# A layer kernel's block products: operands of x, gated features and norm's sums of squares made at other places

## What is computed

```python
xn = rms_norm(x, norm_mix_w)
rq, rk, rv, rg, cq, ckv, kpe, ga, gb = split_columns(xn @ w_in)
ret_y, mla_y, new_state = mixer_core(rq, rk, rv, q, ckv, kpe, w_ukv)
ret_branch = (head_group_norm(ret_y, ret_gn_w).astype(x.dtype) * jax.nn.silu(rg)) @ w_ret_o
mla_branch = mla_y @ w_mla_o
merged = jax.nn.sigmoid(ga) * ret_branch + jax.nn.sigmoid(gb) * mla_branch
h = x + merged @ w_out
g, u = jnp.split(rms_norm(h, norm_ffn_w) @ w_gate_up, 2, axis=-1)
h = h + (jax.nn.silu(g) * u) @ w_down
```

## Time and profile before

| | |
|---|---|
| time, median of 3 runs | 2125.3 us (2124.85 to 2125.86) |
| profiled execution | 2124.33 us, its span 2122.5 us |
| mean granted clock of TensorE in it | 0.970 |
| PE busy | 1985.1 us, 94% of the span |
| DVE, ACT, POOL busy | 1322.6, 799.2, 669.6 us |
| moved by DMA | 302.41 MB, 142 GB/s |

### The profile page before, as it was taken

The page is one execution under the profiler, slowest core; times in us unless marked ns, Lnnn a source line. Parts: engine busy times, 40 slices in busy tenths (PEclk is TensorE's granted clock), DMA queues, the critical chain, the costliest instruction groups (busy, mean ns, idle before and its releaser), DMA issues.

```text
span 2122.5 us, 34897 instructions
## 1 busy us (share of the span) xinstructions
PE 1985.1 (94%) x13994; PEld 1914.6 (90%) x13994; DVE 1322.6 (62%) x1982; ACT 799.2 (38%) x1390; POOL 669.6 (32%) x509
## 2 busy tenths in 40 slices
PE   8989999999897989998999979679999999999997
PEld 8878888789886979998999979679999999999997
DVE  6567776764554645977877897765656565532257
ACT  5334444441232235554554425543444343310010
POOL 0110000001332434755242665844444445200000
PEclk9999999999998999999999989889999999999998
DMA  7301011151343465669655684123232322563412
GB/s 304 109 24 34 21 34 34 32 213 36 137 139 123 157 222 195 245 245 334 219 200 203 206 305 153 46 83 113 94 112 100 106 104 102 220 258 127 168 58 85
DMA packets 121296, 302.41 MB, mean 142 GB/s; under 512 B 14128, under 2 KB 31472, under 8 KB 112944
## 3 DMA queue, kind: packets, MB, share of 16 engines
q1 hardware_dynamic: 121136, 300.18, 40.0%
HBM read 201.88 MB, written 98.25 MB: 141 GB/s over the span
## 4 chain that ended last, share of the span: by engine, by line
PE 69%; DVE 13%; DMA 5%; POOL 4%; issue 4%; ACT 2%; SPq 2%; DVEq 0%; ACTq 0%; POOLq 0%
PE ps L1127 21%; PE ps L1129 21%; PE ps L1128 21%; DVE s_lo L2078 1%; DVE tmp L2085 1%; DVE t_lo L2078 1%; PE ps L1228 1%; PE ps L1320 1%; SPq L1002 1%; PE ps L1222 1%; DVE hg L2440 1%; DVE hg L2432 1%; DVE negmax L2307 1%; DVE hg L2444 1%; DMA xn_lo<-xn_spill 1%
## 5 line engine op out<-in xcount | busy, mean ns | idle before, releaser
L1127 PE MATMUL ps<-s_hi,t_hi 128*128 128x272 f32 x1344 | 393.9, 293 | 25.5 <-DVE s_lo L2078 24.5
L1128 PE MATMUL ps<-s_hi,t_lo 128*128 128x272 f32 x1344 | 393.0, 292 | 0.0
L1129 PE MATMUL ps<-s_lo,t_hi 128*128 128x272 f32 x1344 | 392.1, 292 | 0.0
L1127 PE MATMUL ps<-sx_hi,t_hi 128*128 128x272 f32 x1232 | 358.6, 291 | 23.9 <-DVE hg_r L2078 16.8
L1128 PE MATMUL ps<-sx_hi,t_lo 128*128 128x272 f32 x1232 | 357.6, 290 | 0.0
L1127 PEld LDWEIGHTS ps<-s_hi,t_hi 128*128 128x128 f32 x1344 | 259.3, 193 | 28.6 <-DVE s_lo L2078 22.1
L1129 PEld LDWEIGHTS ps<-s_lo,t_hi 128*128 128x128 f32 x1344 | 258.7, 192 | 0.0
L1128 PEld LDWEIGHTS ps<-s_hi,t_lo 128*128 128x128 f32 x1344 | 258.6, 192 | 0.0
L1127 PEld LDWEIGHTS ps<-sx_hi,t_hi 128*128 128x128 f32 x1232 | 235.8, 191 | 25.0 <-issue 18.8
L1129 PE MATMUL ps<-sx_lo,t_hi 128*128 128x272 f32 x880 | 255.9, 291 | 0.0
L1128 PEld LDWEIGHTS ps<-sx_hi,t_lo 128*128 128x128 f32 x1232 | 235.2, 191 | 0.3 <-issue 0.2
(11 more groups left out here) (275 smaller groups left out, 5026.3 us busy)
## 6 DMA issues: line engine op xcount, KB each, us to landing
t_row<-in_weights SPq DMA_DIRECT2D x48, 512.0 KB, 6.0
y_spill<-hg_r SPq DMA_DIRECT2D x44, 544.0 KB, 3.4
yd<-y_spill SPq DMA_DIRECT2D x22, 1088.0 KB, 6.2
s_raw<-s_x SPq DMA_DIRECT2D x21, 1088.0 KB, 6.0
w_stage<-in_weights SPq DMA_DIRECT2D x35, 512.0 KB, 3.8
raw<-in_weights SPq DMA_DIRECT2D x22, 512.0 KB, 5.1
hg<-in_weights SPq DMA_DIRECT2D x22, 512.0 KB, 5.3
d_stage<-in_weights SPq DMA_DIRECT2D x24, 384.0 KB, 3.0
```

The source lines that it names most:

```text
L1127: nc.tensor.matmul(out, wh, xh, start=start, stop=False, skip_group_check=onto)
L1128: nc.tensor.matmul(out, wl, xh, start=False, stop=False, skip_group_check=onto)
L1129: return nc.tensor.matmul(out, wh, xl, start=False, stop=stop, skip_group_check=onto)
```

## The change

- *Turns of retention.* Turn t loads in chunk 4t; its gains stand behind that chunk's `zs` on ACT (before: ahead of it); POOL's sums are one chunk earlier (4t + 1 and 4t + 2); five of the stores are issued in chunk 4t + 2 and two in 4t + 3. First weights and operand of octet 0 are split behind `zs` or behind the last `zn`, and loaded at chunks 2, 6 and 8 of the last head.
- *GATE_RET's features.* POOL multiplies the blocks C21 and C11, DVE the blocks C22 and C12 (`features_final`). POOL makes their 16 sums at once (`features_sums`), and SP stores them to `s_yg`. `yg_spill`, its reload, and turns 8 to 11 in GATE_A are gone.
- *MIX_OUT's operands.* Steps 0, 1, 2, 3 and 5 are split straight from `hg` and `bm`; only steps 4 and 6 go through `s_m`.
- *FFN norm.* POOL's 14 additions are gone. Each of the 16 squares is summed over partitions by five matmuls of one column into PSUM bank 7 (`square_sums`: 11 squares in MIX_OUT's steps 4 to 6, five in the first pair). DVE adds three partial sums, POOL raises 128x10 values to the power -0.5, DVE spreads them over ten diagonals (`diag_f`), and PE makes rows of them with six matmuls (`norm_rows`), which ACT copies to `res_inv`. Three roots and three reciprocals are gone.

```diff
 ROW_OF_STEP = (0, 0, 4, 4, 2, 1, 3)
...
+def loaded(j):
+    return j < STEPS * MIX_OUT or j % STEPS in (4, 6)
...
+        def operand_turn(o, n):
+            s, p = divmod(n, 4)
+            if o == MIX_OUT and n in (7, 8):
+                return STEPS * o + 3, n - 7
+            if o == MIX_OUT and s == 2 or p not in (1, 2) or (o, s) == (MIX_OUT, STEPS - 1):
+                return None
+            return STEPS * o + s + 1, p - 1
+        def operand_raw(j, part_of):
+            p = 2 * part_of
+            if loaded(j):
+                return s_raw[j % 3][:, p:p + 2, :]
+            s = j % STEPS
...
-            def merged_stores(p, steps):
...
+                    c = (C11, C22, C11, C22, C12, C21, C12)[s]
+                    if name:
+                        sp.wait_ge(m_sum, m_sum_at(o, name, p))
+                        src = bm(c, p)
...
+                        sp.wait_ge(final_p if c in (C21, C11) else final_v, final_at(o, c, p))
+                        src = acc(c, p)
+                    sp.dma_start((s_yg if o == GATE_RET else s_m)[s, :, p, :], src).then_inc(sm_out[s], 16)
...
-            def prep_store(q):
...
+            def prep_store(q, steps):
...
+                else:
+                    sp.wait_ge(prep_in, 32 * q + 32)
+                for s in steps:
+                    if s in (1, 6):
+                        sp.wait_ge(prep_done, 4 * q + 4)
+                    elif s in (2, 5):
+                        sp.wait_ge(prep_done, 4 * q + 2)
+                    src = (prep_tile[0][:, 0:HALF], prep_sum[1], prep_sum[2], prep_tile[1][:, HALF:TOK],
+                           prep_tile[1][:, 0:HALF], prep_sum[0], prep_sum[3])[s]
+                    sp.dma_start(target[s, :, q % 4, :], src).then_inc(prep_out, 16)
...
-                        if at_turn == 0 and turn:
-                            prep_store(turn - 1)
-                        if at_turn == 0 and turn < 8:
+                        if turn < 8 and at_turn == 0:
                             prep_load(turn)
-                        if s[1] == 7 and h == RH - 1:
-                            first_loads()
+                        if turn < 8 and at_turn == 2:
+                            prep_store(turn, (0, 3, 4, 2, 5))
+                        if turn < 8 and at_turn == 3:
+                            prep_store(turn, (1, 6))
+                        if h == RH - 1 and s[1] in (2, 6, 8):
+                            first_loads(s[1])
...
+            def square_sums(i):
...
+                pe.wait_ge(sq_done, i + 1)
+                for a in range(5):
+                    L = P if a < 4 else HALF - 4 * P
+                    last = nc.tensor.matmul(ps[0:L, 7, first + a:first + a + 1], sq[i % 4][:, a * P:a * P + L], ones[:, 0:1],
+                                            start=False, stop=i in (2, 6, 15), skip_group_check=True)
+                last.then_inc(sq_read, 1)
+            def norm_rows(upper):
...
+                pe.wait_ge(inv_done, INV_FFN + 1 + upper)
+                if upper:
...
+                for bank, c0, c1 in ((6, 0, 2 * P), (7, 2 * P, 4 * P), (7, 4 * P, HALF)):
+                    L = min(P, c1 - c0)
+                    last = nc.tensor.matmul(ps[:, bank, c0 % (2 * P) + (2 * P if c0 == 4 * P else 0):][:, 0:c1 - c0],
+                                            ones[0:L, :], diag_f[0:L, HALF * upper + c0:HALF * upper + c1],
+                                            start=True, stop=True)
+                last.then_inc(stat_done, 1)
...
+                        if o == MIX_OUT and s >= 4 and p:
...
+                            for i in ((0,), (1,), (2,), (3, 4), (5,), (6,), (7, 8), (9,), (10,))[3 * (s - 4) + p - 1]:
+                                square_sums(i)
                         octet_unit(o, s, p)
...
+                    if pair == 0 and j == 0:
...
+                        for i in (11, 12, 13):
+                            square_sums(i)
+                    if pair == 0 and j == 3:
+                        for i in (14, 15):
+                            square_sums(i)
+                    if pair == 0 and j in (4, 5):
+                        norm_rows(j - 4)
...
+            def besides(n):
+                if n % 4 == 1 and n < 16:
+                    prep_gains(n // 4)
+                if n == 9 * RH - 3:
+                    for u in range(3):
+                        weights_octet(u)
+                if n == 9 * RH - 1:
+                    for part_of in range(2):
+                        operand_octet(0, part_of)
...
-                        if n % 4 == 1 and n < 16:
-                            prep_gains(n // 4)
-                        if n == 9 * RH - 2:
-                            for u in range(3):
-                                weights_octet(u)
-                        if n == 9 * RH - 1:
-                            for part_of in range(2):
-                                operand_octet(0, part_of)
                         act.wait_ge(z_done, n + 1)
...
                         nc.scalar.activation(zs[n % 2][0:L, :], ps[0:L, 1, 0:DV], ACT.Copy,
                                              scale=z_col[0:L, h, c:c + 1]).then_inc(z_copy, 1)
+                        besides(n)
...
+            def features_final(o, c, p):
+                i = 4 * c + p
+                if o == GATE_RET:
+                    dve.wait_ge(c_act, i + 1)
+                    wait_piece(dve, o, i)
+                    nc.vector.tensor_tensor(acc(c, p), acc(c, p), piece(o, i)[:, :], ALU.mult).then_inc(final_v, 1)
...
+                    late, m = divmod(g - 3, UNITS)
+                    if late == GATE_RET and m >= 20:
+                        features_final(late, (m - 12) // 4, m % 4)
...
+                    dve.wait_ge(sq_read, 16)
+                    nc.vector.tensor_scalar(norm_var, ps[:, 7, NORM_COLUMN:NORM_COLUMN + 10], 1.0 / D_MODEL, EPS,
+                                            ALU.mult, ALU.add).then_inc(var_done, 1)
...
+                    dve.wait_ge(col_done, 4)
+                    for upper in range(2):
+                        for piece_of in range(5):
+                            L = P if piece_of < 4 else HALF - 4 * P
+                            c0 = HALF * upper + P * piece_of
+                            k = 5 * upper + piece_of
+                            ins = nc.vector.tensor_scalar(diag_f[0:L, c0:c0 + L], eye[0:L, 0:L], norm_inv[0:L, k:k + 1],
+                                                          None, ALU.mult)
+                        ins.then_inc(inv_done, 1)
...
-                    for g, (c0, c1) in enumerate(GROUPS):
-                        m = 9 + g
-                        dve.wait_ge(root_done, ROOT_FFN + g + 1)
-                        nc.vector.reciprocal(res_inv[:, c0:c1], ffn_root[m % 2][:, 0:c1 - c0]).then_inc(inv_done, 1)
...
+                    dve.wait_ge(root_done, ROOT_FFN + 1)
+                    gate_scaled(0)
+                    weights_low(1, "B")
+                    dve.wait_ge(root_done, ROOT_FFN + 2)
...
-                        if n % 4 in (2, 3) and n < 32:
-                            prep_sums(n // 4, n % 4 == 3)
+                        if n % 4 in (1, 2) and n < 32:
+                            prep_sums(n // 4, n % 4 == 2)
...
-            def features_gated(i):
+            def features_final(o, i):
...
+            def features_sums(o, name, p):
...
+                    pool.wait_ge(final_p, final_at(o, C11, p))
                     nc.gpsimd.tensor_tensor(bm(C11, p), acc(C11, p), acc(C21, p), ALU.subtract).then_inc(m_sum, 1)
...
+                    pool.wait_ge(final_v, final_at(o, C22, p))
                     nc.gpsimd.tensor_tensor(bm(C21, p), acc(C21, p), acc(C22, p), ALU.add).then_inc(m_sum, 1)
...
+                    pool.wait_ge(m_sum, m_sum_at(o, "S1", p))
                     nc.gpsimd.tensor_tensor(bm(C22, p), bm(C21, p), acc(C11, p), ALU.subtract).then_inc(m_sum, 1)
...
+                    pool.wait_ge(final_v, final_at(o, C12, p))
+                    pool.wait_ge(m_sum, m_sum_at(o, "S2", p))
                     nc.gpsimd.tensor_tensor(bm(C12, p), acc(C12, p), bm(C22, p), ALU.subtract).then_inc(m_sum, 1)
...
-            def squares_added(i):
...
-                nc.gpsimd.tensor_tensor(res_sq[:, c0:c1], res_sq[:, c0:c1], sq[added % 4][:, :], ALU.add).then_inc(sq_sum, 1)
...
-                    late, m = divmod(g - 3, UNITS)
-                    if late == GATE_RET and m >= 12:
-                        features_gated(m - 12)
-                    if late == MIX_OUT and m >= 12 and m not in (12, 16):
...
-                        merged_sums("S2", m - 20)
-                    if late == BRANCH_MLA and 12 <= m < 20:
-                        branches_added(m - 12)
-                    if o == MIX_OUT and n == 21:
-                        pool.wait_ge(oct_done, UNITS * MIX_OUT + 20)
+                    late, m = divmod(g - (3 if g < UNITS * GATE_B else 2), UNITS)
```

(62 more changed lines are left out.)

333 lines of the change are left out of this document (145 added, 188 removed).

## The result

The changed kernel takes 2096.4 us (2096.2 to 2099.2, four runs) against 2125.4 before: a ratio of 0.9867, 95% interval 0.9849 to 0.9884, 29 us faster. I had forecast 2070 in a range that ended at 2096: the direction was right, half of the gain was missing. The profiled execution has a span of 2094.6 us, 27.9 less than before.

What follows compares the result with a forecast made beforehand. PE's matmul work was taken as the bound, busy 1985.1 of 2122.5 us. The terms summed as 2124.3 - 38 + 8 - 8 - 0 - 17 = 2069.3, with the median 1.0 above the profiled run: 2070 us, range 2048 to 2096.

Steps and rivals of the forecast that it cites:

- GATE_RET's features: Around the end of octet 0: added DVE and POOL operations cost 8 us, bounds 0 and 16.
- GATE_A: Turns 8 to 11 leave GATE_A, so PE's waits from 955 to 1054 us go: 8 us gained, bounds 5 and 9.
- MIX_OUT's operands: In MIX_OUT, twenty stores and five loads leave, but PE waits for DVE's `s_lo`: zero gained, bounds 0 and 5.
- the port costs double: Rival, chance 0.18: octet 0's end costs 16 us, giving 2078 us, as DVE is already full.
- the squares eat up the norm's gain: Rival, chance 0.12: each square's matmuls wait 1.1 us for ACT's `sq`, so no norm gain is left: 2087 us.
- Retention: Stores issued ahead of the load free `w_stage`; of 46.2 us loss 38 are gained, bounds 28 and 42.
- 3 for waits that come new: In retention: 3 us kept as loss for new waits, as a gain behind `zs` still precedes ACT's next copies.
- the prediction's half: At clock 0.50 a matmul takes twice its time, so half of PE's busy time there is loss.
- near eight times 1: End of octet 0: basis of the chosen 8 us, between DVE's eight multiplications at 0.71 and at 1.89 us each.
- Norm: FFN norm at MIX_OUT's end and up: 29.6 + 7.0 - 16.7 - 3 = 17 us gained, bounds 8 and 24.
- The gain of 29.6 us of waits: At the start of up: PE's waits for `hg_r` (16.8), `ffn_root` (6.9) and `u` (5.9) all go.
- the 7.0 us of clock loss: Around the FFN norm: PE is busy 14.1 us at clock 0.50, 7.0 of it loss, counted as gained.

Runs made afterwards that it cites:

- the last run above: Kernel before plus new retention turns, fp32r-square norm, two GATE_A turns in GATE_B, and octet 0's first weights' low parts behind the last but one `zn`: 2070.6 us.
- the moved turns: Kernel before with only the new retention turns, plus two of GATE_A's four turns of gated features moved to GATE_B: 2084.9 us, against 2092.3 without the move.

## Why the prediction was wrong, point by point

The forecast of 2070 was 26 us too low. By the stretches about 14 are the norm's, 7 to 8 those of GATE_RET's features and 6 retention's; GATE_A gave 1 more than forecast. The upper end, 2096, stood for two rivals at once, "the port costs double" and "the squares eat up the norm's gain", and this is nearly what came; the second came true in size and not by its mechanism, as PE does not wait for ACT's squares.

**Retention: the mechanism right, 38 forecast, 31.6 in the trace and 33.4 measured alone.** The turn's stores no longer hold `w_stage` back, and the three large waits went. The step that was mis-sized is "3 for waits that come new". Left are, of PE's waits from 539 to 783 us:

```profile
PE ps L1411 <- DVE zn L2437: 5.0, 2, 2.9
PE ps L1400 <- DVE st_f L2420: 4.5, 3, 2.5
PE ps L1148 <- DVE s_lo L2133: 1.5, 2, 0.8
```

That is 11 us, and the prediction's half of the 7.0 us for which PE is busy there at clock 0.50 comes on top: 14.5 are left where 8 were forecast. Of the causes two can be read. The weights of one projection still land late for ACT, and `zs` stands behind them. Then DVE's `zn` takes 2.94 us beside two of the turn's sums on POOL, which the change put into this chunk; 0.4 us is what `zn` takes alone. PE waits 2.9 us for it:

```profile
649.94 1.06 ACT L1580 ACTIVATE w_hi<-w_stage 128x1024 fp32r<-128x1024 f32 x1 [5.70 <-DMA w_stage<-in_weights]
650.90 0.45 ACT L1850 ACTIVATE zs<-ps,z_col 64x256 f32<-64x256 f32 x1
...
654.05 1.32 POOL L2797 TENSOR_TENSOR prep_sum<-prep_tile,prep_tile 128x544 f32<-128x544 f32 x1
654.11 2.94 DVE L2437 TENSOR_SCALAR zn<-zs,mv,rstd 64x256 f32<-64x256 f32 x1 [0.99 <-POOL rstd L2843]
655.34 1.32 POOL L2798 TENSOR_TENSOR prep_sum<-prep_tile 128x544 f32<-128x544 f32 x1
```

And there are DVE's first splits for octet 0. With them moved behind `zn`, in the last run above, the longest wait for `st_f` was 1.7 us. In the changed kernel DVE splits three weights ahead of the last `st_f`, for which PE waits 2.5 us:

```profile
758.03 1.86 DVE L2133 TENSOR_TENSOR t_lo<-t_row,t_hi 128x512 fp32r<-128x512 f32 x3
759.81 0.27 DVE L2420 SCALAR_TENSOR_TENSOR st_f<-ps,columns,dmask 64x64 f32<-64x64 f32 x1
```

**GATE_RET's features: 8 forecast, 15.5 measured.** I had the place, the engine and both ends right, and took the middle. The step that failed is the choice "near eight times 1", with POOL's operations only in the upper bound. The eight multiplications that this choice counts cost about 4 us of PE's time, by the three steps in the run with tiny ones. POOL's 16 sums cost about 17, which the chosen value left out, because POOL itself had slack: 36.93 of 50 us. But a POOL operation costs the time by which it stretches DVE's, and DVE had none to give. So "8" was too low for another reason than its own term; the rival "the port costs double" came true in size, by POOL's sums and not by DVE's multiplications. The rule that I had quoted from the Trainium skill ("SBUF — State Buffer", SBUF: two separate sides), an exclusive lock between VectorE with two SBUF inputs and GpSimd, agrees with these runs (1.79 us for a multiplication beside a POOL operation and 0.71 without, and 0.71 in both cases for the sum with one input in PSUM), and pointed at the 16.

**GATE_A: right, 8 forecast, 9.1 measured**, and 7.4 without the new sums, by the moved turns. The name fits only in part: the waits lie from octet 1's last step on, and 6.4 of the 9.1 us came back in octet 2, GATE_B.

**MIX_OUT's operands: right.** Nothing forecast, 0.0 measured over the stretch. DVE's work there is unchanged and PE waits for the same `s_lo`.

**Norm: 17 forecast, 2.8 measured, 3.3 in the traces.** The cost of the squares was right: between two matmuls of MIX_OUT, 0.125 us apart, five of them take 1.03 us, where 1.05 was forecast:

```profile
1283.58 0.29 PE L1150 MATMUL ps<-s_lo,t_hi 128*128 128x272 f32 x1
1283.70 1.10 PE L1455 MATMUL ps<-ones,sq 128*128 128x1 f32 x10
1284.73 0.40 PE L1148 MATMUL ps<-s_hi,t_hi 128*128 128x272 f32 x1
```

The gain of 29.6 us of waits was right but for two that came new, 4.6 for `diag_f` (3 forecast) and 2.7 for `hg`: PE comes to the squares of the last block before DVE has copied it out. The step that failed is the 7.0 us of clock loss, which I gave back in full. Windows of the changed kernel where the granted clock is 0.50, columns as in the earlier trace rows:

```profile
1301.90:1305.30 3.40, 3.40 (x17) 3.40 (x16) 1.84 (x2) 1.76 (x3) 1.35 (x1) 0.50 0.00 0
1336.00:1346.20 10.20, 9.52 (x45) 9.43 (x46) 8.07 (x7) 5.91 (x9) 5.03 (x4) 0.50 0.08 30
1349.60:1353.10 3.50, 3.50 (x16) 3.50 (x17) 0.00 (x0) 0.00 (x0) 0.00 (x0) 0.51 0.70 245
1363.30:1370.10 6.80, 5.18 (x17) 4.29 (x18) 4.26 (x11) 1.32 (x3) 3.53 (x3) 0.50 0.06 26
sum 23.90, PE 21.59 PEld 20.62 DVE 14.16 ACT 8.98 POOL 9.91; mean PE 5.40 PEld 5.15 DVE 3.54 ACT 2.24 POOL 2.48
```

PE is busy 21.6 us at the lower level (1.2 GHz), more than the 14.1 before; by the prediction's half, 10.8 us of it is loss. The sum with these: 29.6 + 1.0 (a second wait for `ffn_root`) + 7.0 - 10.8 - 16.7 - 4.6 - 2.7 = 2.8. That it meets the median to the tenth is luck. The half is itself a little high: matmuls of 272 columns start 0.227 us apart at the lower level and 0.125 at the higher, so 0.45 of the busy time is loss. With 6.3 and 9.7 in place of 7.0 and 10.8 the sum is 3.2, and the traces give 3.3. Nor is the term fixed: with tiny multiplications, or with all 16 on POOL, the same norm took 3 us less, its stretches at clock 0.50 lying elsewhere.

**MIX_OUT's last steps** show the same on a small scale: 11 squares at 1.05 us are 11.5, with 1.5 (0.45 of 3.4) at the low clock, less a wait of 1.0 for `t_lo` that is gone, make 12.0; 12.5 were lost.

## What to carry to other kernels

Before work goes to an engine that has time, ask which engine it slows there: POOL was busy 39 of 52 us in the window and its sums still cost PE about 17 us, through DVE. When a run takes an operation out, look where in the trace the time came back before the whole difference is put down to it. Work that moves onto the bounding engine costs its full time and what it does to its clock; first halve it by data type, then move it. And when a queue is shared, the cheapest edit is to issue its stores well ahead of the load that waits for them: that, with the work moved around it on ACT, DVE and POOL, was worth more than the whole change.
